# The projections of recurrence heads 0 to 6 made in pairs of seven block products

## Reference

```python
proj = h @ w_in
a_q, a_k, a_v, a_z, g_q, g_f, g_i, g_z = split(proj)
att = chunk_attention(...) * silu(a_z)            # eight heads
q = silu(g_q); k = (1 - lb) * sigmoid(-g_f)
logf = log(lb + (1 - lb) * sigmoid(g_f))
# in chunks: b = cumsum(logf)
#   A[t, s] = sum_d q[t, d] * exp(b[t, d] - b[s, d]) * k[s, d]    for s <= t
#   out = A @ g_i + (q * exp(b)) @ S
#   S = exp(b_last) * S + (k * exp(b_last - b)).T @ g_i
hg = rms(out) * o_g * silu(g_z)
x = x + gate * (concat(att, hg) @ w_out)
```

## Time and profile before

| what | value |
|---|---|
| median of three runs | 1839.52 us (1839.47 to 1839.53) |
| the profiled execution | 1839.64 us, span 1837.8 us |
| TensorE busy | 1831.6 us, 100% of the span |
| VectorE, ScalarE, GpSimd busy | 75%, 48%, 13% |
| granted TensorE clock | full in all slices |
| one paired attention head | 46.2 us |
| one recurrence head | 51.0 us |

### The profile page before, as it was taken

One profiled execution on the slowest core, in us unless ns is written; L12 is line 12 of the kernel. 1 busy time (PEld: TensorE's weight loads), 2 busy tenths in 40 slices (PEclk: granted clock), 3 DMA queues, 4 the chain that ended last, 5 costly groups with the idle time before them and its releaser, 6 DMA issues.

```text
span 1837.8 us, 28086 instructions
## 1 busy us (share of the span) xinstructions
PE 1831.6 (100%) x10006; PEld 1580.8 (86%) x10006; DVE 1380.6 (75%) x2011; ACT 876.1 (48%) x1310; POOL 243.4 (13%) x241
## 2 busy tenths in 40 slices
PE   9999999999999999999999999999999999999999
PEld 8888888888888887888789999998888888888999
DVE  6675678888888878677887777776656666569986
ACT  6543433433343364322556565565455555557333
POOL 3600000000000002444001111100122222110111
PEclk9999999999999999999999999999999999999999
DMA  7344244444454534776336777776222221224442
GB/s 288 110 145 186 86 160 163 160 178 159 163 181 163 181 125 166 247 240 231 118 125 165 185 191 191 190 178 191 92 88 70 91 90 69 91 69 138 150 149 92
DMA packets 68621, 278.25 MB, mean 151 GB/s; under 512 B 7353, under 2 KB 12985, under 8 KB 52289
## 3 DMA queue, kind: packets, MB, share of 16 engines
q1 hardware_dynamic: 60832, 253.08, 40.0%
q0 software_dynamic: 7264, 20.97, 6.4%
q10 hardware_dynamic: 448, 3.17, 0.4%
HBM read 264.85 MB, written 12.35 MB: 151 GB/s over the span
## 4 chain that ended last, share of the span: by engine, by line
PE 94%; DVE 5%; issue 1%; ACT 1%; DVEq 0%; another core or an unknown queue 0%; ACTq 0%
PE ps_p L845 20%; PE ps_p L847 20%; PE ps_p L846 20%; PE ps_p L1234 3%; PE ps_p L1235 3%; PE ps_p L1233 3%; PE ps_o L1010 1%; PE ps_s L1327 1%; PE ps_t L1429 1%; PE ps_t L1430 1%; PE ps_t L1428 1%; PE ps_t L994 1%; PE ps_s L1429 1%; PE ps_s L1428 1%; PE ps_s L1430 1%
## 5 line engine op out<-in xcount | busy, mean ns | idle before, releaser
L845 PE MATMUL ps_p<-act_hi,w_hi 128*128 128x512 f32 x1680 | 672.7, 400 | 0.3 <-DVE w_lo L2125 0.3
L847 PE MATMUL ps_p<-act_hi,w_lo 128*128 128x512 f32 x1680 | 655.9, 390 | 0.0
L846 PE MATMUL ps_p<-act_lo,w_hi 128*128 128x512 f32 x1680 | 654.6, 390 | 0.0
L847 PEld LDWEIGHTS ps_p<-act_hi,w_lo 128*128 128x128 f32 x1680 | 315.4, 188 | 68.7
L845 PEld LDWEIGHTS ps_p<-act_hi,w_hi 128*128 128x128 f32 x1680 | 315.9, 188 | 60.7 <-issue 1.2
L846 PEld LDWEIGHTS ps_p<-act_lo,w_hi 128*128 128x128 f32 x1680 | 316.2, 188 | 59.5 <-issue 0.7
L1452 ACT ACTIVATE w_hi<-raw 128x2048 fp32r<-128x2048 f32 x117 | 223.7, 1912 | 272.1 <-PE ps_p L847 251.6
L2120 DVE TENSOR_TENSOR w_lo<-raw,w_hi 128x2048 fp32r<-128x2048 f32 x115 | 263.8, 2294 | 58.0 <-ACT w_hi L1452 46.5
L2415 DVE CUSTOM_DVE_ANT_0 mkv<-mkv,c_all 128x1024 f32<-128x1024 f32 x96 | 146.2, 1558 | 3.2 <-DVE wk L2162 2.9
L3272 POOL TENSOR_TENSOR ssq_a<-ssq_a,wk 128x512 f32<-128x512 f32 x15 | 36.3, 2420 | 725.1 <-ACT wk L1716 725.1
L1234 PE MATMUL ps_p<-y_lows,w_hi 128*128 128x256 f32 x384 | 109.0, 284 | 0.0
(11 more groups left out here) (521 smaller groups left out, 3575.6 us busy)
## 6 DMA issues: line engine op xcount, KB each, us to landing
raw<-wt_dram SPq DMA_DIRECT2D x122, 1024.0 KB, 4.9
mkv<-ada_dram SPq DMA_DIRECT2D x96, 512.0 KB, 4.6
raw<-wt_dram SPq DMA_DIRECT2D x68, 512.0 KB, 5.4
mkv<-wt_dram POOLq DMA_DIRECT2D x24, 512.0 KB, 7.4
mkv<-wt_dram SPq DMA_DIRECT2D x12, 512.0 KB, 4.7
raw<-wt_dram POOLq DMA_DIRECT2D x12, 512.0 KB, 7.9
qkv<-xT_dram SPq DMA_DIRECT2D x16, 256.0 KB, 2.8
spill_dram<-Y SPq DMA_DIRECT2D x16, 256.0 KB, 2.4
```

The costliest lines, as they stand in the source:

```text
L845: mm(o, wh, hi[:, k, 0:n], start=at == 0, stop=False)
L846: mm(o, wh, lo[:, k, 0:n], start=False, stop=False)
L847: last = mm(o, wl, hi[:, k, 0:n], start=False, stop=at == KT - 1)
```

## The change

Heads 0 to 6 of the recurrence are projected in two pairs each: f with q, then value with z. Head 7 keeps its plain tiles. Their weights use a ring of three half slots, so block n may be split once product n - 3 is done, also from pair to pair. The end of a head (level 7, turns, states, `within`, `across`, output) is put inside the first and second pair of the next head; that of head 6 inside the first plain tile of head 7. Attention head 7 ends inside the first pair of head 0, and some token rows are copied once to buffers that stay free (`keep_tokens`). The scan is made in four pieces of 128 columns instead of one with a row of starts. Outputs of heads go to memory one by one and come back at the end.

```diff
@@ ring of half slots @@
+        HG_FROM = (raw_block(1, 0), raw_block(0, 0), block_sums[1], raw_block(1, 1), raw_block(1, 0), block_sums[1],
+                   raw_block(1, 1))
+        HG_SLOT = (0, 2, 3)
+            return half_slot(HG_SLOT[(7 * (q - ATT_PAIRS) + n) % 3] if q >= ATT_PAIRS else FAST_SLOT[n], t)
         def pair_slot_free(eng, q, n):
 
-            if 3 <= n < 6:
+            if n >= 3 and (q >= ATT_PAIRS or n < 6):
                 eng.wait_ge(product_done.sem, product_done.at("pair", q, n - 2))
+            elif q > ATT_PAIRS:
+                eng.wait_ge(product_done.sem, product_done.at("pair", q - 1, n + 5))
...
@@ TensorE @@
+            def hg_pairs(i):
+                first, second = hg_pair(i, 0), hg_pair(i, 1)
+                if i:
+                    pair_product(first, 0, {1: level(i - 1, NLEV - 1)})
+                    turn_hg(i - 1)()
+                    pair_product(first, 1)
+                    turn_pairs(i - 1)()
+                    pair_product(first, 2, {3: chunk_states(i - 1)})
+                    pair_product(first, 3)
+                    pair_product(first, 4, {3: within(i - 1)})
+                    across(i - 1)()
+                    pair_product(first, 5)
+                    pair_product(first, 6)
+                    pair_product(second, 0, {1: out_sum(i - 1)})
...
+                pair_product(second, 1)
+                pair_product(second, 2, {3: turn_keys(i), 6: level(i, 0)})
+                pair_product(second, 3, {4: level(i, 1)})
+                pair_product(second, 4, {1: level(i, 2), 6: level(i, 3)})
+                pair_product(second, 5, {4: level(i, 4)})
+                pair_product(second, 6, {1: level(i, 5), 6: level(i, 6)})
...
+                hooks = {0: level(i - 1, NLEV - 1), 3: turn_hg(i - 1), 5: turn_pairs(i - 1), 6: chunk_states(i - 1)}
...
@@ ScalarE @@
+            def hg_pairs(i):
+                first, second = hg_pair(i, 0), hg_pair(i, 1)
+                if i:
+                    hg_softplus(i - 1, 3, wk[:, 2, :], wk[:, 3, :])
+                    level_exp(i - 1, NLEV - 1)
+                    first_form(first)
+                    pair_high(first, 3)
+                    hg_turned(i - 1)
+                    hg_sigmoid(i - 1, 3)
...
+                pair_high(second, 0)
+                hg_softplus(i, 1, wk[:, 1, :], hd[:, 0, :])
+                pair_high(second, 1)
+                forgets(i)
+                if i:
+                    out_rows(i - 1)
+                hg_softplus(i, 2, wk[:, 2, :], hq)
+                pair_high(second, 2)
+                hg_sigmoid(i, 2)
+                decay_row(i)
+                pair_high(second, 3)
+                for n in range(3):
+                    level_exp(i, n)
+                first_form(second)
+                diag(i)
+                keys_turned(i)
+                pair_high(second, 4)
+                level_exp(i, 3)
+                level_exp(i, 4)
+                pair_high(second, 5)
+                first_corner(second)
+                level_exp(i, 5)
+                pair_high(second, 6)
+                if i < NHGP - 1:
+                    pair_high(second + 1, 0)
+                    level_exp(i, 6)
+                    pair_high(second + 1, 1)
+                    pair_high(second + 1, 2)
...
@@ VectorE @@
+            def hg_pairs(i):
+                first, second = hg_pair(i, 0), hg_pair(i, 1)
+                if i:
+                    read_pair(first - 1, 4)
+                    value_read(i - 1)
+                    masked(i - 1, NLEV - 3)
+                    pair_lows(i - 1)
+                    masked(i - 1, NLEV - 2)
+                    z_log(i - 1)
+                    pair_low(first, 3)
+                    masked(i - 1, NLEV - 1)
...
+                pair_low(second, 1)
+                forget_in(i, hd[:, 0, :])
+                read_pair(first, 4)
+                pair_low(second, 2)
+                query_log(i, hq)
+                decays(i)
+                for n in range(3):
+                    diff(i, n)
+                queries(i, hq)
+                dve.sem_inc(query_ready.sem, 1)
+                diag_product(i)
+                pair_low(second, 3)
+                if i:
+                    output(i - 1)
+                diag_low(i)
+                read_pair(second, 0)
+                diff(i, 3)
+                masked(i, 0)
+                pair_low(second, 4)
...
```

916 lines of the change are left out of this document (602 added, 314 removed).

## The result

The changed kernel takes 1991.11 us (median of 4 runs, 1989.29 to 1993.58); the kernel before 1839.51 beside it. The ratio is 1.0825, with a 95% interval from 1.0806 to 1.0844: 8.25% slower. The forecast was 1964 with a range of 1930 to 2005. The profiled execution took 1990.67, its span is 1988.9, against 1839.64 and 1837.8 before: 151.1 us more, where the sum said 124.3.

The account below looks back on a forecast made before the run. TensorE, busy 1831.6 of 1837.8 us, was taken as the bound. Waits A 48.6, B 1.8, C 33.4 and D 63.6 make 147.4, less 23.1 saved: 124.3 on 1839.6 gives 1964 us, range 1930 to 2005.

Parts of the forecast that it names:

- Wait A: TensorE's wait for the old head's level 7 in the next head's first product: 7.2 us, 5.4 for head 6.
- Wait C: TensorE's wait before the third product of a head's second pair: 4.9 us a head, 4.0 for head 0.
- S2: The third block product of a head's second pair, or its weight block; TensorE was forecast to wait 4.9 us there.
- Wait D: TensorE's waits from S2 to the last level in the second pair's last product: 9.4 us a head, 7.2 for head 0.
- U: The end of the last product of a head's second pair; level 7 was forecast to go on 7.9 us later.
- B: Stretch from Wait A to the first pair's end: 22.6 us of TensorE work plus a 0.3 us wait a head.
- rival 1: TensorE's clock falls to half in the waits, costing 2.88 us a head in B: 1984 us; chance 0.20.
- What was saved on PE: A head's matmuls fall from 43.6 to 40.3 us, side work stays 7.4: 3.3 less a head, 23.1 in all.
- rival 2: The engines run ahead and TensorE finds its inputs, 47.5 us a head: 1816.5 us; chance 0.06.
- Rival 3: The DMA ring decides, sums in memory arriving late by 2 us a pair: 1844.6 us; chance 0.02.
- Rival 4: Only VectorE's work counts, no hops: Wait D at 5.9, Wait A and Wait C at half; 1901 us; chance 0.12.

Follow-up runs that it names:

- All orders together: All the changes of queue order on ScalarE and VectorE in one kernel, against the changed kernel (1991.1 us): 1901.2 us.
- the third run: Rounding of the second pair's third block put ahead of forget gates, output rows and query's softplus, against the changed kernel: 1986.8 us.
- the fill: 58 matmuls whose sums nothing reads put in TensorE's wait before level 7, against the changed kernel: 1980.8 us.
- the last order: VectorE's queue reordered and levels 1 to 3 later on TensorE, against the kernel with all orders and TensorE's places moved (1901.5 us): 1877.9 us.

## Why the prediction was right, and where its sizes were off

**Direction and mechanism.** That TensorE would lose its cover, and in which places, holds. Waits that the changed kernel did not have to have are shown as the cause by their removal: orders that shorten a chain gave back 4 to 26 us alone, all of them together 113; moving the decays alone gave 3.1, within the uncertainty. The 38 us that are left of the loss no run takes away.

**Wait A** was forecast at 7.2 and 48.6, and is 7.3 and 48.7. Its steps agree within 0.3 us each. Shortening the chain with TensorE's place kept (two runs) left 5.1 and 4.3 of the 7.3; moving the place (one run) took it away for six heads, and half of what that was worth came back elsewhere. All orders together left 2.1, and with the place moved too next to nothing.

**Wait C** was forecast at 4.9 and 4.0, and is 4.85 and 3.5. The reason given, the queue in program order ahead of high S2, is shown by the third run: with that block first (its low part on VectorE too) the wait is gone. What the step left open is that it is not worth its length; 4.4 of 33 us came back.

**Wait D** as a stretch was nearly right (28.3 us from S2 to U against 27.3), its pieces were not. The fourth product's wait for `first_form` was missing: 1.1 a round, and 4.7 in head 0 behind a DMA store. Instead level 0 and the keys' turn wait less than forecast, for TensorE comes to them at half clock. So the stretch agrees in part by luck: the clock and an unforeseen wait stand in for waits that did not come. (The three waits of VectorE in D also add up to 3.4 and not 3.5, which is 0.7 us in all.)

**B** was forecast at 22.6 plus 0.3 and took 24.65. This is the clock: 18 matmuls and the last level at half speed, 1.84.

**The clock, rival 1, is what happened** on top of the waits, and its 1984 is nearer to 1991 than the forecast's 1964. I gave it 0.20 because no row of before showed an idle time of 7 us; it should have had the greater chance, for the forecast itself set waits of 7.2 and 4.9 into each head. Its size in B was put too high: a whole product, 2.88 a head and 20 us for seven heads, where 1.84 a head was measured and the fill gave 10 back. The stretch behind wait C, which it left out, is longer, and filling that wait gave nothing back.

**What was saved on PE** is the step that was mis-sized in its own right. It took 0.120 us a matmul from one product of an attention head without side work in it, and 7.4 for the side work; a round at full clock has 43.1 and 6.4, so 49.5 us a head instead of 47.5. Counted in the same way, the head before has 45.0 for its 192 matmuls (0.234 each, not 0.227) and 6.1. What the sum left out are the 25 places at which a short product is cut by side work or follows another one, 0.19 to 0.34 us where 0.12 was taken. The saving is 1.5 us a head and not 3.3, some 10 us in all and not 23. So rival 2, with every wait gone, would have ended near 1829 and not at 1816, and the point from which the change pays is 1.5 us of waits a head. Even the best order here has 4.

**The difference of 26.8 us** between trace and sum, by rows: a round has 2.0 more of work, 5.4 of half clock (1.9 in B, the rest behind wait C) and 16.8 of waits instead of 21.8, together 2.4 more, 14 in six rounds. Head 0 takes 33.3 us from S2 to U where 25.1 were forecast, with its 4.7 at the fourth product and half clock, 8; the turn of the last attention head's value 1.6; the last head's DMA 1.5. Some 1.5 us stay unexplained. This is an accounting and not a run for each.

**Rival 3**, the DMA ring, showed in no wait of TensorE for a block, in the changed kernel or in the last order; in the last order it showed in ScalarE's (23.1 us in all). Sums in memory landed 7.6 and 6.7 us after issue, as the earlier trace rows had it, under the other waits. **Rival 4**, no hops, falls: it gave 1901, and VectorE is at 44.5 of 72.3 us. Of the two orders that move VectorE's work alone, one moved 3.5 us a head and gained 3, the other 1.4 us a head and gained 13.5; ScalarE's `first_form` waits for that one, and the wait behind it is gone. So it counts what waits for the work, not how much it is.

## What to carry to other kernels

When a change turns one long product that hides a chain into many short ones that alternate with it, count the chain's steps from engine to engine and not the busy shares: here four engines at 94, 74, 47 and 15% lost 150 us. Write each queue in the order of the one chain that ends last: exchanging two calls was worth 16 us, moving 1.4 us of VectorE's work for which another engine waited 13.5, moving 3.5 us of it while ScalarE's queue stayed as it was 3. Moving the place where a chain is awaited helps while other work can cover it and the queues behind it are ready: 28.6 us alone, nothing on top of all the orders until VectorE's queue was changed with it. And where a forecast puts waits of several us on TensorE, the half clock behind them belongs into the sum, not among the rivals.
